# A fused two-block transformer kernel: an idle-product filler at two more places, an own load for the first gains, and a new order of some splits, copies and softmax steps

## What is computed

```
h = rms_norm(x, norm_mix_g);  z = h @ w_in            # 14 column groups
out_a = forgetting_attention(q, k, v, cumsum(log_sigmoid(f))) @ w_fox_up
out_b = (g0 * compressed + g1 * selected + g2 * window attention) @ w_nsa_up
x = x + (sigmoid(g_a) * out_a + sigmoid(g_b) * out_b) @ w_out
x = x + moe(rms_norm(x, norm_ffn_g))                  # top-1 of 4 groups, top-2 of its 4 experts
for l in range(2):                                    # block 2
    p = rms_norm(x, g_pre[l]) @ w_in_2[l]
    o = concat(gated linear recurrence, sliding-window attention), each gated
    x = x + rms_norm(o @ w_out_2[l], g_post[l])
```

## Time and profile before

| | |
|---|---|
| median of 3 runs | 1073.46 us (1073.09 to 1074.45) |
| profiled execution, its own time | 1074.39 us |
| its span, first to last instruction | 1072.6 us |
| busy: TensorE, its weight loads, VectorE, ScalarE, GpSimd | 1023.4, 873.9, 846.1, 657.2, 48.9 us |
| mean granted TensorE clock | 0.990 |
| HBM read | 209.16 MB |

### The profile page before, as it was taken

How to read it: one execution, slowest core, us unless ns; L and a number is a source line. 1 busy time by engine, 2 the same in 40 slices (tenths; PEclk the granted TensorE clock), 3 DMA queues, 4 the chain that set the end, 5 groups by cost and what they waited for, 6 DMA issues and landing times.

```text
span 1072.6 us, 16484 instructions
## 1 busy us (share of the span) xinstructions
PE 1023.4 (95%) x6099; PEld 873.9 (81%) x6099; DVE 846.1 (79%) x1663; ACT 657.2 (61%) x1323; POOL 48.9 (5%) x48
## 2 busy tenths in 40 slices
PE   5989999898999999999989999999998999999997
PEld 4867888886888878888868989888886988988986
DVE  5867977667999999999959677797658877598674
ACT  6455546546888888888835676732446477663352
POOL 0201100002002010010000000000100000000010
PEclk9999999999999999999989999999998999999999
DMA  8533345341999999999944433333344533334220
GB/s 336 195 118 119 119 160 195 118 158 40 384 382 350 366 369 351 386 371 380 358 184 157 158 124 138 117 134 118 121 174 148 185 120 119 119 122 154 93 104 40
DMA packets 30035, 211.32 MB, mean 197 GB/s; under 512 B 3584, under 2 KB 3712, under 8 KB 4992
## 3 DMA queue, kind: packets, MB, share of 16 engines
q1 hardware_dynamic: 28368, 205.01, 51.7%
q10 hardware_dynamic: 1584, 5.21, 1.3%
HBM read 209.16 MB, written 1.05 MB: 196 GB/s over the span
## 4 chain that ended last, share of the span: by engine, by line
PE 58%; DVE 21%; DMA 9%; ACT 8%; issue 3%; POOL 0%; ACTq 0%; DVEq 0%; POOLq 0%; SPq 0%
PE ps L527 14%; PE ps L529 14%; PE ps L528 14%; DVE w_lo L407 11%; DMA ring<-in_panels 8%; PE ps L993 5%; PE ps L532 4%; ACT w_hi L1909 2%; PE ps L676 2%; PE ps L707 1%; ACT s_buf L1955 1%; DVE s_buf L410 1%; DMA prm<-in_prm 1%; PE ps L985 1%; DVE op_rows L407 1%
## 5 line engine op out<-in xcount | busy, mean ns | idle before, releaser
L407 DVE TENSOR_TENSOR w_lo<-ring,w_hi 128x512 fp32r<-128x512 f32 x760 | 481.8, 688 | 93.3 <-ACT w_hi L1909 92.1
L1909 ACT ACTIVATE w_hi<-ring 128x512 fp32r<-128x512 f32 x760 | 424.9, 620 | 166.7 <-PE ps L529 126.8
L527 PE MATMUL ps<-w_hi,op_rows 128*128 128x512 f32 (+2 forms) x800 | 316.3, 395 | 6.9 <-DVE op_rows L1144 2.4
L529 PE MATMUL ps<-w_hi,op_rows 128*128 128x512 f32 (+2 forms) x800 | 309.3, 387 | 0.0
L528 PE MATMUL ps<-w_lo,op_rows 128*128 128x512 f32 (+2 forms) x800 | 308.4, 385 | 0.0
L527 PEld LDWEIGHTS ps<-w_hi,op_rows 128*128 128x128 f32 x800 | 151.8, 190 | 40.1 <-issue 5.9
L529 PEld LDWEIGHTS ps<-w_hi,op_rows 128*128 128x128 f32 x800 | 151.4, 189 | 31.2
L528 PEld LDWEIGHTS ps<-w_lo,op_rows 128*128 128x128 f32 x800 | 152.0, 190 | 27.7
L527 PE MATMUL ps<-op_rows,w_hi 128*128 128x256 f32 x544 | 157.5, 290 | 1.2 <-DVE op_rows L407 1.2
L528 PE MATMUL ps<-op_rows,w_hi 128*128 128x256 f32 x544 | 153.8, 283 | 0.0
L529 PE MATMUL ps<-op_rows,w_lo 128*128 128x256 f32 x544 | 153.7, 283 | 0.0
(11 more groups left out here) (243 smaller groups left out, 1082.3 us busy)
## 6 DMA issues: line engine op xcount, KB each, us to landing
ring<-in_panels SPq DMA_DIRECT2D x194, 1024.0 KB, 6.6
cst<-in_c ACTq DMA_DIRECT2D x1, 1229.0 KB, 7.4
buf_a<-in_pre ACTq DMA_DIRECT2D x2, 512.0 KB, 5.9
keys<-in_post ACTq DMA_DIRECT2D x2, 512.0 KB, 5.5
out<-x_tok SPq DMA_DIRECT2D x2, 512.0 KB, 2.6
cst<-in_c ACTq DMA_DIRECT2D x1, 960.0 KB, 6.8
x_tok<-in_x SPq DMA_DIRECT2D x1, 512.0 KB, 4.8
x_tok<-in_x ACTq DMA_DIRECT2D x1, 512.0 KB, 4.9
```

Source lines behind the costliest of these rows:

```text
L407: return V.tensor_tensor(o, a, b, op)
L527: T.matmul(o, l[0], r[0], start=start, stop=False)
L529: return T.matmul(o, l[1], r[0], start=False, stop=stop)
L1909: return A.activation(o, a, ACT.Copy, scale=scale)
```

## The change

It does these things:

- The gains of the first norm (8 columns of `prm`) come by a load of their own into `g_in`, ahead of the load of `prm`, and the first rows wait for it alone.
- 16 plain f32 matmuls of 128x128 on `ident`, which nothing reads, stand between the wait for `ident` and the first turns.
- In the table, take 11 has `forget` before `fox_norms`, and `log_in` moves from take 13 to take 12.
- `up_split` on DVE stands before the gating product of its take, no longer behind it.
- In the routing, ACT's second Exp stands behind the third copied bank, no longer behind the first.
- At the entry of block 2's first layer the last feed of the experts moves behind the first norm's steps on ACT and DVE, and 4 idle products stand between the turns and the first takes.
- At the entry of its second layer `last_takes` goes through the second half of the tokens k by k with both column halves, feeds move behind `y_add` and `pre_squares`, and 5 idle products stand before the turns and 4 behind them.

```diff
@@ -154,7 +154,7 @@
 
 def beside_block1():
     table = {3: [("lower", 0)], 5: [("fox_sums", 0)], 7: [("fox_norms", 0)], 9: [("fox_sums", 1), ("fox_q", 0)],
-             11: [("fox_norms", 1), ("forget", 0)], 12: [("nsa_gates", 0)], 13: [("log_in", 0), ("fox_k", 0)],
+             11: [("forget", 0), ("fox_norms", 1)], 12: [("log_in", 0), ("nsa_gates", 0)], 13: [("fox_k", 0)],
              20: [("win_sums", 0)], 21: [("win_norms", 0)], 22: [("nsa_side", 0), ("nsa_side", 1)],
              23: [("nsa_side", 2)], 24: [("slc_sums", 0)], 25: [("slc_norms", 0)], 26: [("nsa_side", 3)]}
     at_ticks(table, [(14, 0, None, None), (16, 1, 0, None), (18, 2, 1, 0), (20, 3, 2, 1), (22, None, 3, 2),
@@ -276,6 +276,7 @@
...
+        g_in = sb("g_in", KT)
...
+        ld_gain = sem("ld_gain")
...
@@ -587,17 +589,28 @@
                     token_half(weights_of(t0 + i), i, 1, PIECE, 1, 2 + l, uses)
 
             def last_takes(l, t0):
-                for a in range(TT):
-                    for h in range(2):
-                        for k in range(KT - 4, KT):
-                            w = weights_of(t0 + k - KT + 4, h)
-                            pe.wait_ge(back_lo, 4 * l + k // 2 + 1)
-                            m = mm3(ps[:, 4 + 2 * a + h, :], (hi3[:, k, a * P:(a + 1) * P], lo3[:, k, a * P:(a + 1) * P]),
-                                    w[h], False, k == KT - 1)
-                            if a == 1 and h == 1:
-                                m.then_inc(taken, 1)
-                        if a == 0 or h == 0:
-                            m.then_inc(tail_mm, 1)
+                def product(a, k, h):
+                    w = weights_of(t0 + k - KT + 4, h)
+                    pe.wait_ge(back_lo, 4 * l + k // 2 + 1)
+                    return mm3(ps[:, 4 + 2 * a + h, :], (hi3[:, k, a * P:(a + 1) * P], lo3[:, k, a * P:(a + 1) * P]),
+                               w[h], False, k == KT - 1)
+
+                for h in range(2):
+                    for k in range(KT - 4, KT):
+                        m = product(0, k, h)
+                    m.then_inc(tail_mm, 1)
+                if l + 1 < LAYERS:
+                    for k in range(KT - 4, KT):
+                        product(1, k, 0)
+                        product(1, k, 1).then_inc(taken, 1)
+                    return
+                for h in range(2):
+                    for k in range(KT - 4, KT):
+                        m = product(1, k, h)
+                        if h == 1:
+                            m.then_inc(taken, 1)
+                    if h == 0:
+                        m.then_inc(tail_mm, 1)
 
             def feature_take(t, b, f, n, uses):
                 w = weights_of(t)
@@ -1040,7 +1053,10 @@
                     if name in table:
                         table[name](arg)
 
+
             pe.wait_ge(ld_id, 16)
+            for _ in range(16):
+                T.matmul(ps[:, 1, 0:P], ident[:, :], ident[:, :], start=True, stop=True)
             norm_turns(0)
             for i in range(4):
                 if i == 2:
@@ -1084,7 +1100,10 @@
                 pe.seen = seen
             for l in range(LAYERS):
                 t0, uses = T_L2 + L2_TAKES * l, OUT_L1 + OUT_L2 * l
+                if l:
+                    idle_products(5, 2)
                 pre_turns(l, 0)
+                idle_products(4, 2 if l else 7)
                 first_panel(l, t0, uses)
                 for t in range(t0 + 4, t0 + L_ATT):
                     r = t - t0
@@ -1138,11 +1157,11 @@
                     ts(scr[:, o], x_tok[:, o], stat[:, 2 + a:3 + a], None, ALU.mult).then_inc(norm_x, 1)
 
             def norm_los(a, c):
-                dve.wait_ge(ld_prm, 16)
+                dve.wait_ge(ld_gain, 16)
                 for k in range(4 * c, 4 * c + 4):
                     dve.wait_ge(norm_hi, k // 2 * 2 + 2 if a == 0 else KT + k // 4 * 4 + 4)
                     V.scalar_tensor_tensor(lo3[:, k, a * P:(a + 1) * P], norm_at(a, k),
-                                           prmc("g_mix", k, k + 1), hi3[:, k, a * P:(a + 1) * P].bitcast(F32), ALU.mult,
+                                           g_in[:, k:k + 1], hi3[:, k, a * P:(a + 1) * P].bitcast(F32), ALU.mult,
                                            ALU.subtract).then_inc(norm_lo, 1)
 
             def head_sums(which):
@@ -1609,6 +1628,7 @@
                     if a == 0:
                         pre_sum(0, 0)
                         pre_scale(0, 0)
+                        feed(2 * T_L2 + AHEAD)
                 pre_los(0, 0)
                 pre_sum(0, 1)
                 pre_scale(0, 1)
@@ -1799,7 +1819,7 @@
 
             def behind(t):
                 for name, arg in beside.get(t, ()):
-                    if name in table and name not in ("log_in", "weigh", "scores_out", "qf_bound"):
+                    if name in table and name not in ("log_in", "weigh", "scores_out", "qf_bound", "up_split"):
                         table[name](arg)
 
@@ -1813,6 +1833,7 @@
             feed(8)
             norm_los(1, 0)
             norm_los(1, 1)
+            dve.wait_ge(ld_prm, 16)
             for t in range(T_Z, T_GATE):
                 steps(t)
                 i, step = divmod(t, 4)
@@ -1830,6 +1851,9 @@
             for t in range(T_UP, T_OUT):
                 which, i = divmod(t - T_UP, 4)
                 ahead(t)
+                for name, arg in beside.get(t, ()):
+                    if name == "up_split":
+                        up_split(arg)
                 b = i % 2
                 g = [gates[:, (8 * n + 2 * i) * S:(8 * n + 2 * i + 2) * S] for n in range(2)]
                 dve.wait_ge(gate_on, which + 1)
@@ -1865,7 +1889,6 @@
                 seen = dict(dve.seen)
                 full_pass()
                 dve.seen = seen
-            feed(2 * T_L2 + AHEAD)
             combine()
             for l in range(LAYERS):
                 t0, tok = T_L2 + L2_TAKES * l, TOK_L1 + TOK_L2 * l
@@ -1880,16 +1903,16 @@
                     behind(t)
                 t1 = t0 + L2_TAKES
                 y_sums(l, 0)
-                feed(2 * t1 + 3)
                 y_add(l, 0)
                 if l + 1 == LAYERS:
                     y_sums(l, 1)
                     y_add(l, 1)
                     return
+                feed(2 * t1 + 3)
+                pre_sum(l + 1, 0)
                 feed(2 * t1 + 4)
-                pre_sum(l + 1, 0)
+                pre_scale(l + 1, 0)
                 feed(2 * t1 + 5)
-                pre_scale(l + 1, 0)
                 y_part(l, 1, 0)
                 y_sum(l, 1)
                 pre_los(l + 1, 0)
@@ -1922,10 +1945,10 @@
                              accum_out=stat[:, a:a + 1]).then_inc(norm_sq, 1)
 
             def norm_his(a, c):
-                act.wait_ge(ld_prm, 16)
+                act.wait_ge(ld_gain, 16)
                 for k in range(4 * c, 4 * c + 4):
                     act.wait_ge(norm_T, k // 2 + 1 if a == 0 else 4 + k // 4 + 1)
-                    copy(hi3[:, k, a * P:(a + 1) * P], norm_at(a, k), prmc("g_mix", k, k + 1)).then_inc(norm_hi, 1)
+                    copy(hi3[:, k, a * P:(a + 1) * P], norm_at(a, k), g_in[:, k:k + 1]).then_inc(norm_hi, 1)
 
             def forget_log(_):
                 la = stat[:, 96:112]
@@ -2050,7 +2073,7 @@
                     act.wait_ge(row_mm, k + 1)
                     copy(rin[:, k, :, :], ps[:, 3 + k % 4, :].rearrange("p (g n) -> p g n", g=4),
                          prmc("g_ffn", k, k + 1)).then_inc(rows, 1)
-                    if k == 0:
+                    if k == 2:
                         act.wait_ge(soft_in, 2)
                         A.activation(pe_, pe_, ACT.Exp).then_inc(soft_e, 1)
                     if k % 2:
@@ -2129,8 +2152,8 @@
 
             def y_squares(l, a):
                 for b in (2 * a, 2 * a + 1):
-                    if b < 3:
-                        act.wait_ge(tail_mm, 3 * l + b + 1)
+                    if b < (2 if l + 1 < LAYERS else 3):
+                        act.wait_ge(tail_mm, 2 * l + b + 1)
                     else:
                         act.wait_ge(taken, T_L2 + L2_TAKES * (l + 1))
                     A.activation(buf_d[:, b * 512:(b + 1) * 512], ps[:, 4 + b, :], ACT.Square, scale=D ** -0.5,
@@ -2170,6 +2193,7 @@
 
             nc.scalar.dma_start(x3[:, 0, :], x_in[0, 0:P, :]).then_inc(ld_x, 16)
             nc.scalar.dma_start(ident[:, :], c0_in).then_inc(ld_id, 16)
+            nc.scalar.dma_start(g_in[:, :], prm_in[:, PRM["g_mix"][0]:PRM["g_mix"][1]]).then_inc(ld_gain, 16)
             nc.scalar.dma_start(prm[:, :], prm_in).then_inc(ld_prm, 16)
             act.wait_ge(pool_step, 1)
             ac(A.activation(stat[:, 4:5], minus_half[:, 0:1], ACT.Square))
@@ -2182,6 +2206,7 @@
             feed(8)
             norm_his(1, 0)
             norm_his(1, 1)
+            act.wait_ge(ld_prm, 16)
             nc.scalar.dma_start(cst[:, 0:C1_W], c1_in).then_inc(ld_c1, 16)
             for l in range(LAYERS):
```

(3 more changed lines are left out.)

## The result

The changed kernel takes 1066.07 us (median of 4 runs, 1065.13 to 1067.51); the kernel before, run beside it, 1073.95. The ratio is 0.9927, 95% interval 0.991 to 0.9944: 7.9 us faster, where 4.95 were forecast. The profiled execution has a span of 1064.9 us, 7.7 less than before. The kernel with the same text, profiled once more (the last experiment), was 9.0 less.

The account below looks back on a forecast made before the run. TensorE, busy 273.33 of 274.80 us in the expert stage, was taken as the bound. 2.0 - 1.75 - 1.2 - 1.7 + 0.45 - 2.75 = -4.95 from 1073.46 gave 1068.5 us (own range 1067.1 to 1069.7, wide 1065.5 to 1071.6).

Parts of the forecast that it names:

- the wide range: Whole kernel: 1065.5 to 1071.6 us, meant to hold all but some 2 in 10.
- Rival (1): Clock rises early at both fillers: start +1.5, block 2's first entry 0.0, sum -5.9, 1067.5 us; chance 0.17.
- its stretched form: Rival (1) with -3.5 at the second entry and a still sooner clock rise at the first: 1065.5 us.
- Start, forecast +2.0: Kernel start: 16 products delay ACT's copies by 3.4 us, 1.4 of it slack; loss 2.0, bounds +1.5 and +3.0.
- Forget gate, -1.75: TensorE's 2.80 us wait for `log_in` shrinks as Ln and `log_in` come earlier; gain 1.75, between 1.1 and 2.8.
- Nsa split, -1.2: Nsa products: splits start at 204.35, so TensorE's 1.21 us wait for the first goes; gain 1.2.
- Routing, -1.7: ACT copies the second and third bank while the second Exp's input is awaited; gain 1.7, bounds -1.2 and -2.0.
- First entry, +0.45: Block 2's first entry: nothing won ahead of the turns; idle products +0.87, earlier clock -0.42; bounds +0.9 and -1.5.
- the branch explains the start as well, and nothing in the change shortens it: Block 2's first entry: TensorE's 6.75 us branch, until 550.35, holds the turns at 550.42; nothing won ahead of them.
- Second entry, -2.75: Block 2's second entry: `y_add` comes 3.7 us earlier, the first take 2.75 earlier; bounds -1.5 and -3.5.
- Experts, 0: Expert stage: the sum had no term for it; a length change over 2 us would prove the forecast wrong.
- Rival (2): Expert stage takes the early gains back: -2.65 ahead is lost, -2.3 stays, 1071.2 us; chance 0.11.

Follow-up runs that it names:

- experiment 1: The changed kernel without the 16 products on `ident` ahead of the first turns: 1063.73 us, ratio 0.9903 to the kernel before.
- experiment 7: The changed kernel with 22 products on zeroed `cst` ahead of the wait for `ident` and 10 behind the first turns, replacing the 16: 1060.24 us, ratio 0.9881.
- experiment 8: The changed kernel with `up_split` behind the take again and the second Exp ahead of ACT's copy of bank 1 again: 1070.38 us, ratio 0.9975.
- experiment 4: The changed kernel with the feed of block 2's first panels back ahead of the branches on DVE and ACT: 1066.42 us, ratio 0.9922.
- experiment 5: The changed kernel without the idle products at block 2's two entries: 1069.7 us, ratio 0.9959.
- experiment 6: The changed kernel with the old order of feeds and sums ahead of block 2's second entry on DVE and ACT: 1068.52 us, ratio 0.9958.

## Why the prediction was right, and where its sizes were off

The change is faster, as forecast, because the waits at which it aims were real and mostly went. That the total came out within the wide range is in part luck: two clock terms that the sum lacked or had too small, at the picks and at the first entry, gave 1.4 and some 1.1 more, and one at the gate took 1.6 away. At the start and the second entry the result lies at what Rival (1) and its stretched form had (+1.5 and -3.5; measured +1.6 and -3.4), not at the forecast itself.

**Start, forecast +2.0: +1.57, mechanism right.** 32 records on `ident`, two per product, then the copies, then take 2: all as forecast, each some 0.4 earlier, since the 16 products took 5.8 us and not 6.1. In nine executions with this start they took 5.2 to 6.5 and the start lost 1.00 to 2.40. That agrees with the Trainium skill, "TensorE: Matmul & The Clock Gate", Part 1, by which the change comes at another moment from run to run.

**Forget gate, -1.75: the size at the scores right, the sum wrong.** The scores come 1.64 earlier behind the start's shift. But I priced what is left of the wait by its length alone. The two waits, 2.80 and 0.73, became one of 1.98 us; in five of the seven traces with this place unaltered and the filler of the change ahead of it (and in experiments 1 and 7, with another start), the clock fell there and the score products took about 1.6 more, so nothing stayed. In the other two, and with the wait filled, the 1.64 stayed. The edit still looks good: with the old table the fall costs more (+2.33), though that is one trace.

**Nsa split, -1.2: -1.5.** Undone, it gives 1.5 back; the first product waits for nothing, and 1.4 of it comes at that product.

**Routing, -1.7: -3.0.** The Exp's part is -1.60, as forecast, and it spares the draw behind that wait (experiment 8). The other 1.40 is the clock at the picks, 1.00 for 0.50 around 250, where six idle products took 2.74 us before and 1.64 now; no edit of the routing did it. It held in ten of the traces with the change and fell in three (experiments 4, 5 and 6). My sum had no such term, neither here nor, with the other sign, at the gate.

**First entry, +0.45: -1.53. Here a step failed**: "the branch explains the start as well, and nothing in the change shortens it". The branch did hold the turns, but the moved feed shortened it, from 6.75 to 4.18 us. It ended at 545.1, 0.8 behind the last products, and the turns came at 546.58. They no longer wait for it but for DVE's rows, and these for ACT's squares, which begin at 543.46, 1.9 us after DVE has written the x that they square; the profile shows nothing else for which ACT waited. That the branch loads instructions which stand behind the panels is what the packets speak for (experiment 4); a load alone was not measured.

For the time that step was worth nothing, though. From the last output product the turns gained 1.1 (-2.73 there, -3.84 at the turns), and the first product lost it again behind DVE's two pieces of the same moved feed (-2.70): so far the place gives 0.0. The whole -1.5 comes behind it (-4.27 at 571) and is the clock, 1.00 for 0.50, for which the sum had 0.42; that is the term that was sized wrong. The idle products were forecast to cost 0.87; DVE's rows end later than they do, so here they cost nothing. With the feed late the place gives -1.5 to -2.1 in the six traces where the clock held and -0.5 to +0.9 in three with fillers where it fell; in a fourth (experiment 8) the low stretch lay mostly in a wait.

**Second entry, -2.75: -3.38; a right sum from a wrong cause.** I put it down to the feeds' order on DVE and ACT. That is 0.7. The last takes' order, which I hardly spoke of, is 1.3: it gives the panels back one by one, and ACT's copies start 2 us earlier. The remaining 1.4 was not split. Most of it lies ahead of the turns, where TensorE stands still: of the 3.38, 3.18 is there at the turns, and behind the first product only 0.3 comes, since short waits take the place of the slow products of before. Each order was undone with the other in place, and both undone together was not run, so part of the 1.4 may be what they cover for each other. In the one trace without fillers the entry keeps all 3.4; by the times of experiment 5 that may not hold for other executions.

**Experts, 0: +0.28.** That is two things: the stage itself is 0.9 longer, and 0.6 comes back at the output products, here and in every other trace of the changed kind; what released it was not looked for. Rival (2) falls: the stage took 272.6 to 277.4 us whether it began at 255.7 or at 265.7, without a trend. But this spread alone is larger than most terms, and it is most of what separates two traces of one kernel.

## What to carry to other kernels

Fill only time that the work does not need: a filler has to begin with the wait and end with it, and the best place for the first one is ahead of the first load. A wait of about 2 us on TensorE costs its length and sometimes the slow products behind it, so price both and treat the second as a draw. A short wait is no safeguard: before, the clock fell at the picks although TensorE's longest wait in the 6 us ahead of it was 0.5. One profile of a kernel shows one such draw, so hold it against the granted clocks of all its runs. When only one place is in question, compare the lateness between two points around it, since the stage beside it may vary by more than the edit gives, and look where a ring's buffers are given back before reordering those who fill it.
